# Raw fp32 products for the first four w_in pieces, a load of its own for the condition vector, and an earlier last feed-forward modulation

## The reference, cut to what matters

```python
c_act = jax.nn.silu(c)
for l in range(DEPTH):                        # 2 layers, 256 tokens, width 1024
    mod = (c_act @ ada_w[l] + ada_b[l])[:, None, :]
    sh1, sc1, g1, sh2, sc2, g2 = jnp.split(mod, 6, axis=-1)
    h = rmsnorm(x, norm_mix_w[l]) * (1.0 + sc1) + sh1
    x = x + g1 * hybrid_mixer(h, ...)         # proj = h @ w_in, groups f, q, ab, ac, ah, i, v, u, g ...
    h = rmsnorm(x, norm_ffn_w[l]) * (1.0 + sc2) + sh2
    x = x + g2 * (swiglu(h, ...) if l == 0 else moe_swiglu(h, ...))
return rmsnorm(x, final_norm_w)
```

## Time and profile before

| | us |
|---|---|
| median of 3 runs | 1587.91 (1587.69 to 1589.39) |
| profiled execution, device time | 1589.61 |
| span of its trace (first to last instruction) | 1586.9 |
| TensorE busy in it | 1528.8 |
| VectorE busy | 1294.7 |
| ScalarE busy | 957.9 |
| mean granted TensorE clock, share of full | 0.978 |

### The profile page before, as it was taken

How to read it: one execution, slowest core, us unless ns; L and a number is a source line. 1 busy time by engine, 2 the same in 40 slices (tenths; PEclk the granted TensorE clock), 3 DMA queues, 4 the chain that set the end, 5 groups by cost and what they waited for, 6 DMA issues and landing times.

```text
span 1586.9 us, 26455 instructions
## 1 busy us (share of the span) xinstructions
PE 1528.8 (96%) x9638; PEld 1322.0 (83%) x9638; DVE 1294.7 (82%) x1508; ACT 957.9 (60%) x1104; POOL 39.5 (2%) x46
## 2 busy tenths in 40 slices
PE   6899999899999899999889999999999999999997
PEld 5898999899999898999877777777777777777775
DVE  7776878767764878868669989899899998989897
ACT  3434544444433533544368777787878777787784
POOL 0000000000000000000002000000000000000200
PEclk7899999999999999999979999999999999999999
DMA  9943878468976543789549999999999999999993
GB/s 348 295 143 107 264 254 287 152 194 293 305 300 196 167 144 128 259 287 375 194 124 385 395 388 396 383 377 370 382 364 388 372 379 381 363 386 368 392 391 147
DMA packets 260624, 469.00 MB, mean 296 GB/s; under 512 B 15732, under 2 KB 129580, under 8 KB 260548
## 3 DMA queue, kind: packets, MB, share of 16 engines
q1 hardware_dynamic: 257024, 456.75, 81.3%
q0 software_dynamic: 3248, 11.11, 1.9%
q10 hardware_dynamic: 276, 0.09, 0.0%
HBM read 453.90 MB, written 14.00 MB: 295 GB/s over the span
## 4 chain that ended last, share of the span: by engine, by line
PE 75%; DVE 4%; issue 1%; ACT 0%; DVEq 0%
PE psU L621 52%; PE psA L621 22%; PE psA L1033 1%; DVE split L1332 1%; DVE merged L1441 0%; PE psU L971 0%; PE psU L993 0%; DVE rstd L1437 0%; DVE split L1813 0%; DVE adacc L1404 0%; DVE sc L1567 0%; DVE work L1635 0%; DVE work L2017 0%; DVE work L1551 0%; DVE work L1544 0%
## 5 line engine op out<-in xcount | busy, mean ns | idle before, releaser
L1116 ACT ACTIVATE split<-raw 128x1024 fp32r<-128x1024 f32 x754 | 787.5, 1059 | 364.8 <-PE psU L621 180.3
L1813 DVE TENSOR_TENSOR split<-raw,split 128x1024 fp32r<-128x1024 f32 x528 | 615.2, 1219 | 22.7 <-ACT split L1116 20.7
L621 PE MATMUL psU<-hS,split 128*128 128x256 f32 x3936 | 490.2, 287 | 18.1 <-DVE hS L1518 14.7
L621 PEld LDWEIGHTS psU<-hS,split 128*128 128x128 f32 x3936 | 483.5, 195 | 20.9 <-issue 16.8
L621 PE MATMUL psU<-split,xE 128*104 128x512 f32 (+1 forms) x2304 | 498.1, 376 | 2.3 <-DVE xE L1940 2.3
L621 PEld LDWEIGHTS psU<-split,xE 128*104 128x104 f32 x2304 | 366.9, 168 | 120.2 <-issue 2.4
L1332 DVE TENSOR_TENSOR split<-raw,split 128x1024 fp32r<-128x1024 f32 x226 | 268.8, 1218 | 67.3 <-ACT split L1116 66.9
L621 PE MATMUL psA<-split,hidE 128*104 128x512 f32 x1056 | 249.2, 395 | 0.0
L621 PEld LDWEIGHTS psA<-split,hidE 128*104 128x104 f32 x1056 | 175.4, 168 | 63.9
L1404 DVE SCALAR_TENSOR_TENSOR adacc<-raw,cact,adacc 128x1024 f32<-128x1024 f32 x70 | 89.7, 1281 | 4.1
L621 PE MATMUL psU<-yS,split 128*128 128x256 f32 x576 | 70.1, 283 | 0.0
(11 more groups left out here) (241 smaller groups left out, 806.8 us busy)
## 6 DMA issues: line engine op xcount, KB each, us to landing
raw<-in_moe_w_dram SPq DMA_DIRECT2D x528, 512.0 KB, 7.0
raw<-in_w_in_dram SPq DMA_DIRECT2D x120, 512.0 KB, 5.9
raw<-in_ada_w_dram SPq DMA_DIRECT2D x96, 512.0 KB, 7.1
raw<-in_ffn_w_dram SPq DMA_DIRECT2D x66, 512.0 KB, 6.4
raw<-in_w_o_dram SPq DMA_DIRECT2D x16, 512.0 KB, 9.1
token_rows<-sc SPq DMA_DIRECT2D x10, 512.0 KB, 9.5
raw<-in_w_br_a_dram SPq DMA_DIRECT2D x8, 512.0 KB, 8.7
raw<-in_w_br_c_dram SPq DMA_DIRECT2D x8, 512.0 KB, 9.2
```

The source lines that it names most:

```text
L621: return pe.matmul(o, a, b, start=start, stop=stop, skip_group_check=True)
L1116: return act.activation(o, i, ACT.Copy)
L1813: TTN(split[:, slot, 1, :], raw[:, (RAW0 + n) % RAW, :], split[:, slot, 0, :].bitcast(F32), ALU.subtract).then_inc(s_lo, 1)
```

## The change

The condition vector gets its own load, first on ACT's queue, its own transpose and its own unit ("c"); the other small vectors are transposed after x. The squares of x move ahead of the lower-bound sigmoid on ACT, the lower-bound arithmetic moves down on DVE. Pieces 8 to 11 are no longer split: TensorE multiplies the raw piece by `merged` (h in plain fp32), one fp32 product in place of three fp32r products, and releases the piece by a semaphore of its own, `s_wused`. The high and low parts of these first four chunks of h are made later, from `merged`, for the groups behind. The two halves of a section get separate banks of one event, so that sc1 and sh1 don't wait for each other. `DIRECT` changes: in the second half both pieces 14 and 15 of sc1 are multiplied directly, and all four of sh1 go through DVE. The look-ahead count `used` of f0 falls from 5 to 1 because four split pieces are gone; it still ends with pieces 28 and 29. `modulate(FFN_ADA[-1])` moves into the iteration f = 20 of DVE's feed-forward loop.

```diff
-DIRECT = [(1, 0, 2), (0, 0, 2), (1, 1, 3), (0, 1, 3)]
+DIRECT = [(1, 0, 2), (0, 0, 2), (1, 1, 2), (1, 1, 3)]
...
 
-    plan = [(("vec", 0), "A")] + [(("x", j), "A") for j in range(4)]
+    plan = [("c", "D")] + [(("x", j), "A") for j in range(4)] + [(("vec", 0), "A")]
...
-            plan += [(("half", 1, 0), "D"), ((0, "norm1"), "A")]
-            plan += [(("half", 0, 0), "D"), (("half", 1, 1), "D"), (("half", 0, 1), "D")]
+            plan += [((0, "norm1"), "A"), (("half", 0), "D"), (("half", 1), "D")]
...
-            used += 5 if (kind, key[2]) == (START_GROUPS[0], 0) else 1
+            used += 1
...
-        out += [("split", "w_in", 0, h * 512, COLS[g] + 256 * j, 256) for g in START_GROUPS for j in range(2)]
+        out += [("split" if h else ("whole", 2 * n + j), "w_in", 0, h * 512, COLS[g] + 256 * j, 256)
+                for n, g in enumerate(START_GROUPS) for j in range(2)]
...
+                elif use[0] == "whole":
+                    sp.wait_ge(s_wused, use[1] + 1)
...
+            def half_section(s, h):
...
                 acc = ada1 if s else adacc
...
+                bank = psA[2 * (EVENT_AT["half", h] % 2) + 1 - s]
+                first = True
+                pe.wait_ge(s_uD, emptied(UNITS, UNIT_AT["c"], "D"))
+                for n, piece in enumerate(DIRECT):
+                    if piece[:2] == (s, h):
+                        pos, p = MOD_POS[n], piece[2]
+                        pe.wait_ge(s_raw[pos % RAW], 16 * (pos // RAW + 1))
+                        for kk in range(2):
+                            for m in range(4):
+                                last = mm(bank[:, m:m + 1], raw[:, pos % RAW, (4 * kk + m) * P:(4 * kk + m + 1) * P],
+                                          cact[:, 2 * p + kk:2 * p + kk + 1], first, False)
+                                first = False
+                        last.then_inc(s_mpc, 1)
+                pe.wait_ge(s_afree, max(i for i, piece in enumerate(PRODUCTS) if piece[:2] == (s, h)) + 1)
+                for m in range(4):
+                    last = mm(bank[:, m:m + 1], acc[:, (4 * h + m) * P:(4 * h + m + 1) * P], ones[:, 0:1],
+                              first, m == 3)
+                    first = False
+                last.then_inc(s_half if s else s_ev, 1)
...
+                for n, key in enumerate(keys):
+                    banks.append(open_unit(key))
+                    pos = WHOLE_POS[n]
+                    pe.wait_ge(s_raw[pos % RAW], 16 * (pos // RAW + 1))
+                    for m in range(2):
+                        for k in range(4):
+                            if n == 0 and m == 0 and k % 2 == 0:
+                                pe.wait_ge(s_hf, k // 2 + 1)
+                            last = mm(banks[n][:, m * T:(m + 1) * T], raw[:, pos % RAW, k * 256 + m * P:k * 256 + (m + 1) * P],
+                                      merged[:, k, :], m == 0 and k == 0, False)
+                    last.then_inc(s_wused, 1)
+                    if n == 2:
+                        open_event(("half", 1))
+                        half_section(1, 1)
+                half_section(0, 1)
+                for n, key in enumerate(keys):
+                    w = next_split()
+                    for m in range(2):
+                        for kk in range(4):
+                            if n == 0 and m == 0 and kk % 2 == 0:
+                                pe.wait_ge(s_h, 2 + kk // 2 + 1)
+                            last = tile(banks[n][:, m * T:(m + 1) * T], w, 4 + kk, kk * 256 + m * P, False, kk == 3)
+                    last.then_inc(s_used, 1)
...
-                    ada_half(1, 0)
-                    row_factors()
-                    ada_half(0, 0)
+                    bank, _ = open_event((0, "norm1"))
+                    open_event(("half", 0))
+                    half_section(1, 0)
+                    row_factors(bank)
+                    half_section(0, 0)
                     start_units()
...
-            pe.wait_ge(s_small, 16 * len(stacks))
...
+            pe.wait_ge(s_c, 16)
+            pe.transpose(open_unit("c")[:, 0:KD], stackC[0:KD, :], ident[0:KD, 0:KD]).then_inc(s_unit, 1)
...
+            pe.wait_ge(s_small, 16 * len(stacks))
...
+            act.dma_start(stackC[0:KD, :], c.rearrange("b (r p) -> (b r) p", p=P)).then_inc(s_c, 16)
...
+            act.activation(cact[:, :], unit("c")[:, 0:KD], ACT.Sigmoid).then_inc(s_cact, 1)
+            for j in range(4):
+                copy(xT[:, 2 * j:2 * j + 2, :].rearrange("p a b -> p (a b)"), unit(("x", j))[:, :]).then_inc(s_uA, 1)
             copy(vecs[:, :], unit(("vec", 0))[:, 0:NA_ROWS + NB_ROWS]).then_inc(s_uA, 1)
...
+            act.wait_ge(s_x, 16)
+            for tt in range(TT):
+                link(act.activation(work[:, 6 + tt, :], xrow[:, tt, :], ACT.Square, accum_out=vst[:, tt:tt + 1]))
...
-                    high_parts(4 * h + 1)
-                    act.wait_ge(s_eD, emptied(EVENTS, EVENT_AT["half", 0, h], "D"))
+                    high_parts(h)
+                    act.wait_ge(s_eD, emptied(EVENTS, EVENT_AT["half", h], "D"))
...
-                        ins = act.activation(hS[:, 0, k, :], merged[:, k, :], ACT.Identity, bias=mod[:, 0, k:k + 1])
+                        ins = act.activation(hS[:, 0, k, :] if h else merged[:, k, :], merged[:, k, :], ACT.Identity,
+                                             bias=mod[:, 0, k:k + 1])
                         if k % 2:
-                            ins.then_inc(s_hh, 1)
-                    high_parts(4)
+                            ins.then_inc(s_hh if h else s_hf, 1)
+                    for k in (0, 2) if h == 0 else ():
+                        act.wait_ge(s_hf, k // 2 + 1)
+                        copy(hS[:, 0, k:k + 2, :].rearrange("p a b -> p (a b)"),
+                             merged[:, k:k + 2, :].rearrange("p a b -> p (a b)")).then_inc(s_hh, 1)
+                high_parts(4)
...
+            TTN(cact[:, :], cact[:, :], unit("c")[:, 0:KD], ALU.mult).then_inc(s_uD, 1)
...
-                bank = event(("half", s, h))[0]
+                if s:
+                    dve.wait_ge(s_half, h + 1)
+                    bank = psA[2 * (EVENT_AT["half", h] % 2)]
+                else:
+                    bank = event(("half", h))[1]
...
-                start_products(range(3))
+                start_products(range(2))
+                dve.wait_ge(s_uA, 5)
+                TTN(lbs[:, 1, 1, :], vecs[:, LB_ROW + HB:LB_ROW + 2 * HB], vecs[:, LB_ROW:LB_ROW + HB],
+                    ALU.subtract).then_inc(s_lbsig, 1)
+                start_products(range(2, 5))
                 dve.wait_ge(s_rms, 1)
                 link(dve.reciprocal(vst[:, 4:6], vst[:, 2:4]))
                 settle()
                 link(TS(factor[:, 0, :], ones[:, :], vst[:, 4:5], None, ALU.mult))
                 settle()
                 TS(factor[:, 1, :], ones[:, :], vst[:, 5:6], None, ALU.mult).then_inc(s_rdiag, 1)
-                start_products(range(3, 5))
+                start_products([5])
                 modulate_half(1, 0)
                 dve.wait_ge(s_eA, emptied(EVENTS, EVENT_AT[(0, "norm1")], "A"))
-                dve.wait_ge(s_uA, 5)
                 start_chunks(0)
-                start_products([5])
                 modulate_half(0, 0)
-                low_parts(1)
-                norm_low(0, 0, 0)
-                norm_low(0, 0, 2)
-                low_parts(4)
-                start_products(range(6, 11))
+                lower_bounds()
+                start_products(range(6, 8))
+                for k in (0, 2):
+                    dve.wait_ge(s_hh, k // 2 + 1)
+                    TTN(hS[:, 1, k:k + 2, :].rearrange("p a b -> p (a b)"), merged[:, k:k + 2, :].rearrange("p a b -> p (a b)"),
+                        hS[:, 0, k:k + 2, :].rearrange("p a b -> p (a b)").bitcast(F32), ALU.subtract).then_inc(s_h, 1)
+                start_products(range(8, 11))
                 modulate_half(1, 1)
                 start_chunks(1)
                 start_products([11])
                 modulate_half(0, 1)
-                low_parts(5)
+                low_parts(1)
...
                 bank = unit(("ffn", f))
+                if f == NF - 2:
+                    modulate(FFN_ADA[-1])
...
-            modulate(FFN_ADA[-1])
```

More of the change, by code:

```diff
@@ L233 @@
 START_ADA = len(PRODUCTS)
+WHOLE_POS = [pos for pos, p in enumerate(PIECES) if p[0][0] == "whole"]
 MORE_AT = next(pos for pos, p in enumerate(PIECES) if p[0][0] == "ada") + 1
@@ L690, in ada_sum @@
                 last.then_inc(s_unit if s in DOWN_ADA else s_ev, 1)
-            def ada_half(s, h):
+            def half_section(s, h):
                 acc = ada1 if s else adacc
[L695 to L704, removed]
-                    return last
-                def direct(first):
-                    pe.wait_ge(s_cact, 1)
-                    pe.wait_ge(s_cm, 1)
-                    pe.wait_ge(s_raw[pos % RAW], 16 * (pos // RAW + 1))
-                    for kk in range(2):
```

(36 more changed lines are left out.)

47 lines of the change are left out of this document (23 added, 24 removed).

## The result

The changed kernel takes 1599.08 us, median of 7 runs (1594.84 to 1600.5), beside 1588.85 for the kernel before: ratio 1.0061, interval 1.0048 to 1.0074. It is slower, by 9.7 us by that ratio. Its profiled execution took 1600.5, span 1598.7, the upper end of its runs. The forecast was 1597.1.

What follows compares the result with a forecast made beforehand. TensorE, busy 96% of the span, was taken as the bound. Start +13.3 and seam -4.1 gave +9.2 on the profiled 1589.61, so 1598.8, and 1597.1 for the median of runs; range 1587 to 1602.

Steps and rivals of the forecast that it cites:

- T: End of the fourth raw unit on TensorE in the start, forecast at 51.6 us, between 41.8 and 54.4.
- The start, first half: Products begin when piece 0 lands and separate banks remove a 1.67 us wait; wide matmuls start at 25.2, 4.2 us sooner.
- The second half: Second half of the start: first three units end at 38.5, narrow matmuls at 45.4, fourth unit at 51.6.
- The narrow stretch: 40 narrow instructions before the fourth unit: clock falls after 2.5 us, 20 at 0.12 and 20 at 0.22, end 45.4.
- The wait: SP holds piece 22 and all behind it until the fourth raw unit ends; ab begins 28.2 us later, at 79.8.
- The price of the cold start of ab: TensorE, idle from about 73, runs 5.3 us at half clock when ab begins: 2.65 us more.
- The start in sum: The later begin of ab, 10.6 us, and its half-clock stretch, 2.65: the start costs 13.3 us.
- The seam: Feed-forward seam: modulation moved up saves 2.4 us idle and 1.7 of half clock, -4.1, at least -2.4.
- The end: Behind the start TensorE is busy nearly without a gap, so nothing gives the loss back; whole change +9.2 us.
- Rival 1: Start: loads behind piece 22 come in time and only TensorE's chain counts, 1579.3 us; chance 0.12.
- Rival 2: Start: wait exists but clock holds through narrow matmuls or rises sooner, fourth unit ends 42 to 45; 1587.5 to 1590.5; chance 0.17.
- 8.5 us of ACT's and DVE's own work: Between f0's second sigmoid and ab: gates, low or high parts, products and q0's product, 8.5 us that comes again.

Runs made afterwards that it cites:

- the kernel with q first: The changed kernel with DVE's two gated products of q ahead of two products of ada piece 2: 1595.59 us, ratio 1.0046 to the kernel before.
- the seam alone: The kernel before with only the last feed-forward modulation moved up: 1584.89 us, ratio 0.9976.
- the fastest kernel: The changed kernel with raw pieces outside the ring, small loads behind ab's first two pieces, and q's products earlier on DVE: 1580.76 us, ratio 0.9951; repeat 1582.29.

## Why the prediction was right

The sign, the mechanism and the time came out. The size did so partly by luck, because misses of both signs cancelled: T was put too late, the wait behind it too short, and the end of the kernel at nothing. By the steps:

- **The start, first half**: wide matmuls were put at 25.2 and came at 24.66. The banks and the condition do what was said.
- **The second half**: the first three units were to end at 38.5 and ended at 38.2. The narrow stretch let the clock fall, 2.8 us in rather than 2.5, and it ended at 43.8 and not 45.4; the fourth unit took 5.6 and not 6.2. So T was 49.4 and not 51.6, 2.2 too late in the forecast. The three other profiles of the same start have T at 46.1 to 46.5, 5 us sooner than forecast, so the one of the changed kernel is the one that flatters the forecast. This term was the worst sized. The first units' end was 0.3 of the 2.2, the narrow stretch 1.3 and the fourth unit 0.6: of the 40 narrow instructions I had 20 at full clock at 0.12, and in fact some 25 ran at 0.11 (32 of them take 3.6 us at full clock in the kernel with q first), and then 15 at 0.20 and not 20 at 0.22.
- **The wait**: from T to ab I had 28.2 and it was 30.0. Its parts: four pieces 1.8 (2.0), small loads 5.9 (6.5), piece 28 issued at T + 8.6 by my spacing and at T + 10.4 in fact, since the two ada pieces took 1.75 and not 0.91; ACT could split 29 at T + 18.5, not T + 16.3; ACT's reading 3.4 (3.5), and 8.5 for the rest, which was 8.0. So the issues were too cheap by 1.7 and the landing by 0.5. Both prices came from rows of one place of the kernel before.
- **The price of the cold start of ab**: 2.65 forecast, 8.57 - 6.01 = 2.56 measured.
- **The start in sum**: +13.3 forecast; ab's first unit ends 12.7 later (87.9 against 75.2), the last pair of the feed-forward 12.9 later.
- **The seam**: -4.1 forecast; 12.9 - 9.75, -3.1, in the trace of after, -3.2 in that of the seam alone, and -3.8 in the runs. The idle time was 2.4 as forecast. The clock gave some 1.5 of its 1.7, but the down matmuls then ran at a slower pace, which took 1.0 back and for which I had nothing (last section).
- **The end**: +9.2 forecast on the profiled execution, +9.75 at the xE line, +10.9 for its whole time (1600.5 against 1589.61). Behind xE I had nothing: the loop of the experts is 0.67 longer, the wait before the last scatter 0.4, and that scatter ran at half clock, 5.37 against 3.67, of which 1.0 reaches the end. That is 11.8, the difference of the spans (1598.7 and 1586.9); outside the span the changed kernel takes 1.8 where the one before took 2.7, which leaves 10.9. Where these parts are is shown; why they are there I can't explain (below).

Rival 1, that the loads come in time, asked for piece 29 within 7 us of T; it came 18.5 after, and every trace with the hold has ab at T + 26 or more. Rival 2, that the wait is there but the clock holds, is partly what the other profiles show: T is near 46 in them, between my 51.6 and its 42 to 45, and the runs reach down to 1594.8. It was right to leave it a chance; in no trace did T fall below 45.6 (46.1 with the start as it is in the changed kernel). What I had not priced is the second wait, on DVE in front of ab, as a thing of its own: it sat in the "8.5 us of ACT's and DVE's own work" that comes again, of which 2.7 are an order that could be changed.

## What to carry over

A queue that issues in order is held by its oldest unmet release, so a buffer that is freed later, by a consumer standing behind other work, delays all that is issued behind it; before such a change, list the pieces behind it in the ring, and everything that shares the queue, down to the small loads. One wait added to the old kernel tests this ahead of any redesign: here it showed a loss as large as the whole. And where a stall is removed, read the next engine's own order at that place: two products that nobody waited for stood in front of the one that TensorE needed.

## What the runs showed of the hardware

**The granted clock moves at other times in other executions of the same code.** The same raw start begins at 24.66 in the changed kernel and at 24.57 in the one with q first. Stretches of the changed kernel (the clock is the third number from the end):

```profile
28.00:30.00 2.00, 2.00 (x6) 1.55 (x6) 1.57 (x3) 0.00 (x0) 0.00 (x0) 0.50 1.06 388
...
42.00:44.00 2.00, 2.00 (x11) 2.00 (x11) 0.00 (x0) 0.00 (x0) 0.00 (x0) 0.50 0.00 0
44.00:46.00 2.00, 2.00 (x5) 1.64 (x6) 1.91 (x6) 0.00 (x0) 0.00 (x0) 0.50 0.00 0
46.00:48.00 2.00, 2.00 (x7) 1.59 (x7) 1.50 (x3) 0.00 (x0) 0.00 (x0) 0.59 0.00 0
```

and of the other:

```profile
28.00:30.00 2.00, 2.00 (x11) 1.77 (x10) 1.46 (x3) 0.00 (x0) 0.00 (x0) 1.00 1.06 388
...
42.00:44.00 2.00, 2.00 (x6) 1.64 (x5) 1.97 (x6) 0.00 (x0) 0.00 (x0) 0.50 0.00 0
44.00:46.00 2.00, 2.00 (x8) 1.63 (x7) 0.69 (x1) 0.00 (x0) 0.00 (x0) 0.77 0.00 0
```

In the one the clock is at its lower level (1.2 GHz) until about 30.6, full (2.4 GHz) to about 40.8 and low again for 6.8 us; in the other it is full before 28, and low for 3.4 us only. That is 3 us of T, and so more than half of what the runs of the changed kernel spread by (5.7). In the one it falls in the stretch of one-column matmuls, in the other just behind it, and TensorE shows no idle time in either.

**The same matmuls run at different paces, all at full clock.** In the down matmuls three instructions take 0.352 us before (8 groups of three from 470.02 to 472.84) and 0.360 with the seam moved (469.98 to 472.86). The first and the last of each; before:

```profile
470.02 0.40 PE L621 MATMUL psA<-hid_hi,split 128*128 128x256 f32 x2
...
472.84 0.40 PE L621 MATMUL psA<-hid_hi,split 128*128 128x256 f32 x2
```

the seam alone:

```profile
469.98 0.40 PE L621 MATMUL psA<-hid_hi,split 128*128 128x256 f32 x2
...
472.86 0.40 PE L621 MATMUL psA<-hid_hi,split 128*128 128x256 f32 x2
```

The difference lasts for the first 140 groups or so. In the kernel with the seam moved these matmuls lead by 1.47 us at the tenth group, which is what the clock brought, and by 0.48 at the 140th: 1.0 us is lost again, about the 0.9 by which the seam gave less than idle and clock together. The engine never idles there and the granted clock is 1.00 in both. Each of the thirteen traces keeps one pace through this stretch: 0.352 in the three whose modulation stands at its old place, 0.360 in six of those where it is moved, 0.356 in the other four. What sets the pace no run tells.

**A plain fp32 product is cheaper than I had it.** In the changed kernel 24 instructions of the raw units start from 32.83 to 38.01, when the next kind begins: 0.22 each at full clock and 0.43 a product, where three fp32r passes are 0.365. The Trainium skill, page "FP8 and Floating Point Precision", section "TensorE Precision Notes", says that true fp32 makes four passes. With the fp32r pass of 0.122 as the price of each, my estimate by that page is 0.49 a product, some 13% above the measured 0.43. The page gives a number of passes and no time, so this trace doesn't contradict it: what is too dear is the price of a pass, taken from fp32r rows.

**Left open.** The loop of the experts (from xE to the last scatter's transposes) takes 757.3 us in all nine traces with the changed start and 756.6 in the four without it, and the wait before the last scatter is 1.74 in those nine and 1.35 in the four. There DVE's addition begins 0.68 us behind the start of the last transposes in the fastest kernel and 0.30 behind it in the one with the seam alone. The scatter behind it ran at half clock in five of those nine and in none of the four. The code of these places is the same, and no run tells why. So 1.1 to 2.1 us of what the raw start costs lie at the far end of the kernel, and may be part of why its 3 us don't show in the times, though 0.3 to 1 us of it come back outside the span (1.7 to 1.8 us in every run with the changed start, 2.1 to 2.8 in nearly all others). Nor does any run take away ACT's look-ahead, by which f0 can't be read before piece 29 is split. The traces show ACT idle there for a DMA, but that a shorter look-ahead would have won the loss back is argued and not shown.
